# Where the remainder of the token rows is formed, and where the selection of expert slots is built, in a four-layer diffusion trunk step

## What is computed

```python
pg = softmax(xt @ w_rg); p_grp, g_idx = top_k(pg, 1)            # 1 of 4 groups
le = (xt @ w_re) of that group; pe_top, e_idx = top_k(softmax(le), 2)
weight = p_grp * pe_top / sum(pe_top)
hid = silu(xt @ w1[x]) * (xt @ w3[x])
y = sum over experts of (hid * combine) @ w2[x]
```

## Time and profile before

| | |
|---|---|
| median of 3 runs | 1474.15 us (1473.59 to 1474.91) |
| profiled execution | 1473.45 us, of which the span from the first to the last instruction is 1471.7 us |
| TensorE | busy 1370.5 us (93% of the span), mean granted clock 0.981 |
| VectorE, ScalarE, GpSimd | busy 373.4 us (25%), 287.7 us (20%), 61.2 us (4%) |
| transfers | 552.48 MB, 375 GB/s over the span |
| chain that ended last | PE 76%, DMA 18%, DVE 4%, ACT 1%, issue 1% |

### The profile page before, as it was taken

How to read it: one execution, slowest core, us unless ns; L and a number is a source line. 1 busy time by engine, 2 the same in 40 slices (tenths; PEclk the granted TensorE clock), 3 DMA queues, 4 the chain that set the end, 5 groups by cost and what they waited for, 6 DMA issues and landing times.

```text
span 1471.7 us, 17304 instructions
## 1 busy us (share of the span) xinstructions
PE 1370.5 (93%) x7218; PEld 740.3 (50%) x7218; DVE 373.4 (25%) x885; ACT 287.7 (20%) x519; POOL 61.2 (4%) x54
## 2 busy tenths in 40 slices
PE   6999998999989999989999889899999886999986
PEld 3686574444335888754444346544443343444433
DVE  2343514111103322351111121421111134111112
ACT  3211023111102232231111113411110143111102
POOL 1001311000000000020000000200000011000000
PEclk9999999999999999999999999999999997999999
DMA  9945998999999942697999999979999999999994
GB/s 381 419 160 195 404 404 320 384 425 428 428 427 422 421 162 100 277 409 292 428 426 427 428 423 420 421 312 412 426 428 428 425 420 424 428 428 428 425 428 175
DMA packets 54213, 552.48 MB, mean 375 GB/s; under 512 B 5937, under 2 KB 7921, under 8 KB 8817
## 3 DMA queue, kind: packets, MB, share of 16 engines
q1 hardware_dynamic: 52496, 549.29, 89.8%
q10 hardware_dynamic: 1634, 2.02, 0.4%
HBM read 549.19 MB, written 2.10 MB: 375 GB/s over the span
## 4 chain that ended last, share of the span: by engine, by line
PE 76%; DMA 18%; DVE 4%; ACT 1%; issue 1%; POOL 0%; SPq 0%; DVEq 0%; POOLq 0%
PE bank L713 23%; DMA ring<-in_moe_w 16%; PE bank L659 13%; PE bank L737 11%; PE bank L678 4%; PE bank L619 4%; PE bank L696 3%; DMA ring<-in_w_ada 2%; PE bank L492 2%; PE bank L508 2%; PE bank L633 2%; PE bank L833 1%; PE bank L934 1%; PE bank L995 1%; PE bank L569 1%; PE bank L565 1%
## 5 line engine op out<-in xcount | busy, mean ns | idle before, releaser
L713 PE MATMUL bank<-ring,arena 128*64 128x512 f32 x1024 | 230.7, 599 | 31.1 <-DMA ring<-in_moe_w 30.3
L713 PE MATMUL bank<-ring,hT 128*64 128x512 f32 x1024 | 225.3, 594 | 0.0
L737 PE MATMUL bank<-ring,arena 128*64 128x512 f32 x896 | 198.9, 596 | 0.0
L713 PEld LDWEIGHTS bank<-ring,arena 128*64 128x64 f32 x1024 | 73.3, 137 | 180.7 <-issue 150.4
L713 PEld LDWEIGHTS bank<-ring,hT 128*64 128x64 f32 x1024 | 72.1, 137 | 139.3 <-issue 137.3
L1398 DVE TENSOR_TENSOR rows<-rows,bank 128x512 f32<-128x512 f32 x32 | 22.0, 688 | 468.8 <-PE bank L713 468.8
L737 PEld LDWEIGHTS bank<-ring,arena 128*64 128x64 f32 x896 | 61.2, 137 | 117.7 <-issue 112.3
L659 PE MATMUL bank<-hT,ring 128*128 128x256 f32 x512 | 113.4, 384 | 1.7 <-DVE hT L1366 1.7
L659 PEld LDWEIGHTS bank<-hT,ring 128*128 128x128 f32 x512 | 97.8, 192 | 16.0 <-issue 2.7
L1132 ACT ACTIVATE yv_big<-bank,arena 128x512 fp32r<-128x512 f32 x64 | 44.0, 688 | 287.5 <-PE bank L737 287.5
L619 PE MATMUL bank<-ring,condT 128*32 128x512 f32 x768 | 91.8, 606 | 8.2 <-DMA ring<-in_w_ada 6.5
(11 more groups left out here) (213 smaller groups left out, 1273.2 us busy)
## 6 DMA issues: line engine op xcount, KB each, us to landing
ring<-in_moe_w SPq DMA_DIRECT2D x166, 2048.0 KB, 19.2
ring<-in_w_ada SPq DMA_DIRECT2D x96, 1024.0 KB, 21.3
ring<-in_moe_w SPq DMA_DIRECT2D x36, 1024.0 KB, 19.5
arena<-in_moe_w SPq DMA_DIRECT2D x16, 1024.0 KB, 16.8
ring<-in_hy_w_in SPq DMA_DIRECT2D x12, 1024.0 KB, 26.2
ring<-in_hy_w_out SPq DMA_DIRECT2D x4, 1024.0 KB, 12.1
ring<-in_gla_w_v SPq DMA_DIRECT2D x4, 1024.0 KB, 27.8
ring<-in_gla_w_g SPq DMA_DIRECT2D x4, 1024.0 KB, 26.5
```

Source lines behind the costliest of these rows:

```text
L713: last = mm(bank[4 + kind][SLOTS * e:SLOTS * e + SLOTS, :], x[:, k, at:at + SLOTS], w[:, kk, e, :], start=k == 0, stop=k == KD - 1)
L737: last = mm(bank[6 + q // 2][SLOTS * e:SLOTS * e + SLOTS, :], hidT[:, f, SLOTS * e:SLOTS * e + SLOTS], w[:, ff, e, :], start=f == 0, stop= ...
```

## The change

Per layer:

- TensorE writes the transposes as an open accumulation on each bank. After ScalarE has written `htok_big` (one copy of each bank instead of two), TensorE multiplies it by a negated identity `minus` onto the same bank, which leaves bank - big = rest. ScalarE copies the four banks into `htok_rest`. GpSimd's `token_rests` and `htok_raw` are gone. ScalarE builds `minus` once a layer, in `residual`.
- TensorE's four ada pieces are split: two ahead of the rests, one after them, one after the rank matmuls.
- VectorE takes up the ranks directly after `memb` and builds the selection from them; the weights (L1498 to L1507) follow it. The table of slot numbers runs from 1 to 64 instead of 0 to 63, which makes the subtraction of 1 (L1512) superfluous.
- ScalarE's two small exponentials stand behind the first rest copy and behind the last.

```diff
-    base = np.concatenate([np.eye(P), np.tile(np.arange(SLOTS), (P, 1)),
+    base = np.concatenate([np.eye(P), np.tile(np.arange(1, SLOTS + 1), (P, 1)),
...
-        htok_raw = ar(2048, G, D)
+        minus = exact("minus", 5120, P)
... TensorE, moe
-                        last = tr(bank[2 * g + k // 4][:, (k % 4) * P:(k % 4) * P + P], hT[:, k, g], ident)
+                        last = mm(bank[2 * g + k // 4][:, (k % 4) * P:(k % 4) * P + P], hT[:, k, g], ident,
+                                  start=k % 4 == 0, stop=k % 4 == 3, is_transpose=True, skip_group_check=True)
...
-                    ada(beside, 4, 8)
+                    ada(beside, 4, 6)
+                for n in range(4):
+                    pe.wait_ge(s("htok_big"), 4 * i + n + 1)
+                    mm(bank[n][:], minus[:], htok[0][:, n // 2, (n % 2) * 512:(n % 2) * 512 + 512], start=False,
+                       stop=True, skip_group_check=True).then_inc(s("rest_mm"), 1)
+                if beside is not None:
+                    ada(beside, 6, 7)
                 pe.wait_ge(s("members"), i + 1)
...
                 mm(bank[4][:, 32:48], ones16[:], mb[1], start=False, stop=True).then_inc(s("ranks_mm"), 1)
+                if beside is not None:
+                    ada(beside, 7, 8)
                 pe.wait_ge(s("htok_rest"), 4 * (i + 1))
... ScalarE, residual (m == 0)
+                        act.wait_ge(s("base_loaded"), 16)
+                        act_fn(minus[:], ident, ACT.Copy, scale=-1.0)
... ScalarE, moe
-                        for dst in (htok_raw, htok[0]):
-                            last = act_fn(dst[:, g, h * 512:h * 512 + 512], bank[2 * g + h][:], ACT.Copy)
-                        last.then_inc(s("htok_big"), 1)
-
-                    act.wait_ge(s("route_in"), 2 * i + g + 1)
-                    act_fn(*route_exp[g], ACT.Exp).then_inc(s("route_exp"), 1)
+                        act_fn(htok[0][:, g, h * 512:h * 512 + 512], bank[2 * g + h][:], ACT.Copy) \
+                            .then_inc(s("htok_big"), 1)
+                for n in range(4):
+                    act.wait_ge(s("rest_mm"), 4 * i + n + 1)
+                    act_fn(htok[1][:, n // 2, (n % 2) * 512:(n % 2) * 512 + 512], bank[n][:], ACT.Copy) \
+                        .then_inc(s("htok_rest"), 1)
+                    if n == 0:
+                        act.wait_ge(s("route_in"), 2 * i + 1)
+                        act_fn(*route_exp[0], ACT.Exp).then_inc(s("route_exp"), 1)
+                act.wait_ge(s("route_in"), 2 * i + 2)
+                act_fn(*route_exp[1], ACT.Exp).then_inc(s("route_exp"), 1)
... VectorE, moe: these lines move ahead of the weights
+                dve.wait_ge(s("ranks_mm"), i + 1)
+                v.reduce_max(r_mx, bank[4][:, 32:48], AX.X)
+                chain(stt(rank[:], bank[4][:, 0:32].rearrange("p (g e) -> p g e", g=G), 1.0, memb, ALU.add, ALU.mult))
+                build_sel("", 0)
...
-                chain(ts(rank[:], r_rk, -1.0, None, ALU.add))
... GpSimd
-            token_rests(0)
```

More of the change, by code:

```diff
@@ L1507, in moe @@
                          r_wt.unsqueeze(2).broadcast_to([P, G, 4, 4]), ALU.mult))
-                dve.wait_ge(s("ranks_mm"), i + 1)
-                v.reduce_max(r_mx, bank[4][:, 32:48], AX.X)
-                chain(stt(r_rk, bank[4][:, 0:32].rearrange("p (g e) -> p g e", g=G), 1.0, memb, ALU.add, ALU.mult))
-                chain(ts(rank[:], r_rk, -1.0, None, ALU.add))
-                build_sel("", 0)
                 for j in range(3):
@@ L1773, in add_squares @@
                     v.tensor_tensor(hT[:, 0], hT[:, 0], hT[:, k], ALU.add).then_inc(s("squares_added"), 1)
[L1775 to L1781, removed]
             pool.wait_ge(s("skip_loaded"), 16)
@@ L1793, in _ @@
             add_squares(1)
-            token_rests(0)
             add_squares(3)
-            token_rests(1)
             add_squares(5)
-            token_rests(2)
             add_squares(7)
-            token_rests(3)
 def vector_columns(inputs):
```

## The result

The changed kernel takes 1455.1 us (median of 4 runs, 1454.46 to 1455.64) against 1474.53 us for the kernel before beside it: a ratio of 0.9866, with a 95% interval of 0.9852 to 0.9879. The forecast was 1454.8 in a range of 1450 to 1462.5. The profiled execution took 1455.36 us.

What follows compares the result with a forecast made beforehand. The weight stream was taken to set the late pace, with DMA gaps behind routing in layers 0 to 2. Gains of 6.2, 6.4 and 6.7 us, together 19.3, take 1473.45 to 1454.1, plus 0.7: 1454.8 us, range 1450 to 1462.5.

Steps and rivals of the forecast that it cites:

- GpSimd's remainders: VectorE's chain to the membership: four long operations shorten once GpSimd's remainders go, membership 3.49 us earlier.
- The price of 0.17 us for a free operation: VectorE's long operations with two SBUF operands, 0.76 to 1.24 us, priced at 0.17 us without GpSimd's work beside them.
- TensorE's own work: Rest matmuls and ada pieces ahead of the ranks: rests about 0.9 us, third piece ending with the membership, 0.1 us added.
- Selection before weights: VectorE behind the rank matmuls: selection first and no L1512; with the earlier membership, layer 0's gather starts 4.8 us earlier.
- The clock: TensorE's gather: full clock instead of half, 4.0 us long, gaining 1.4, 1.6 and 1.9 us in layers 0 to 2.
- The stream: Weight transfers: gains fit the DMA gaps behind routing in layers 0 to 2; layer 3, without a gap, gains 0.
- The rival that layer 3 pays too: Layer 3's routing gain also reaches the end: 4 layers, about 26 us, 1448 us; chance 0.05.
- The rival that the stream absorbs everything: DMA gaps behind the routing have another cause than the full ring, so no gain: 1474 us; chance 0.03.
- that of another cause of the stall: VectorE's stall isn't GpSimd's; only its order counts, about 3 us in all, 1471 us; chance 0.06.
- that of late rests: Rest matmuls and ScalarE copies on the transposed banks end last, gather 4.7 us late, 1488 us; chance 0.02.
- The sum: Whole kernel: 6.2, 6.4 and 6.7 us in layers 0 to 2, 0 in layer 3, together 19.3 us.

Runs made afterwards that it cites:

- run with reads alone: Changed kernel, with GpSimd again doing four unused 128x512 subtractions beside VectorE's chain in each layer (also called the run with subtractions): 1465.64 us, ratio 0.9945.
- run with memsets: Changed kernel, with GpSimd doing eight 128x512 memsets into an unused tile beside VectorE's chain: 1455.93 us, ratio 0.9873.
- run without tie-breaking: Changed kernel, with each choice of a maximum cut from four VectorE operations to one, so equal scores would choose two: 1455.25 us, ratio 0.9862.
- the rests alone: Changed kernel with the weights ahead of the selection again and slot numbers from 0, the remainders still on TensorE: 1464.85 us, ratio 0.9934.
- the order alone: Kernel before, with only the selection built ahead of the weights from slot numbers 1 to 64; GpSimd still forms the remainders: 1469.77 us, ratio 0.9969.
- the same with two pieces moved: Changed kernel without tie-breaking and with the matmuls of two ada pieces moved, seven between the router's logit matmuls, one behind the transposes: 1455.04 us, ratio 0.9863.
- the run that fills the wait: Kernel before, with TensorE filling its wait for the membership with 15 zero matmuls (30 in layer 3): 1471.71 us, ratio 0.9982.
- the run that delayed it by 3.6 us: Changed kernel with GpSimd's four unused subtractions in layer 3 alone: 1456.6 us, ratio 0.9874.

## Why the prediction was right

**GpSimd's remainders.** Forecast 3.49 us off the membership; measured 9.39 - 5.91 = 3.48 in layer 0, and the same in layers 1 and 2. The price of 0.17 us for a free operation, read from the same line after GpSimd's end, carried it. The run with reads alone brought the stall back without the rest of the old kernel, and the run with memsets did not: together they show the cause.

**TensorE's own work.** This is the term that was too small. I had the ranks start at 6.02; they start at 6.28. The four rests took 1.13 us from 231.49 to the third piece at 232.62, not 0.9. Their spacing was as priced, 0.23 to 0.24 us, but there are 0.33 us behind the first and 0.32 behind the last. The ada pieces around them took a little more, too: the two ahead 1.85 instead of 1.82, the third 1.00 to the ranks instead of 0.91. I wrote that TensorE would be ready just when the membership comes, within 0.1 us. It is 0.37 us late, and the run without tie-breaking shows that it, and not VectorE, sets the time there.

**Selection before weights.** From the start of the ranks to the selection I had 1.32 us, and it is 1.32. Alone, the order brought the gather 1.35 to 1.38 us forward in each of the three layers, against the 1.36 of the forecast, and the median 4.7 us down, 1.6 a layer. One thing I had missed: in its place behind the rest copies, ScalarE's second exponential holds up the weights by 1.0 us, as the run with the rests alone shows. The new order hides it.

**The clock.** Taken as full, and in layers 0 to 2 it was: 4.05 us in the gather, forecast 4.0. From the gather's start to the first expert matmul that is 1.33, 1.51 and 1.84 us less, forecast 1.4, 1.6 and 1.9. In layer 3, where the prediction looked for the same on TensorE, it was not: 0.50 and 5.44 us. It cost nothing there, because nothing in that layer's routing reaches the end. The full clock was also less safe than I had it. In all profiles the clock was full in every gather with 0.2 us of idle time ahead of it. With 1.18 us it fell in most (all four layers of the order alone, layer 3 of the changed kernel) but not in all (layer 3 without tie-breaking, and the same with two pieces moved: 4.05 and 4.06 us), and with 2.3 to 2.5 us it fell in all layers of the rests alone and in two of four in the run that fills the wait. In layers 0 and 2 of the run with subtractions it was at 0.50 though no idle time stood just ahead: it had fallen in the wait for the membership. So the idle time just ahead doesn't decide by itself.

**The stream.** Each layer's gain fitted into the DMA gap behind its routing, and layer 3 gained nothing, to 0.01 us. In all fourteen profiles its experts start between 9.96 and 18.51 us after its first transpose, and from there to the last long piece it is 236.2 to 236.8 us in thirteen of them and 237.3 in one; the earliest and the latest start both have 236.26. The rival that layer 3 pays too fell with that and with the run that delayed it by 3.6 us. The rival that the stream absorbs everything fell with the gaps' going; that of another cause of the stall with the run with reads; that of late rests with the last rest at 6.84, 0.76 us ahead of the selection.

**The sum.** 18.3 us in the three layers against the forecast 19.3: 0.27 us a layer by TensorE's late ranks, 0.07 by the gather. The medians differ by 19.4 us and the profiled executions by 18.1; the start-up was 0.94 us shorter in the profile after, its end 0.9 us longer. So that the forecast is within 0.3 us of the median is in part luck: the sum was 1 us too large, and about 1 us of scatter made up for it.

## What to carry to other kernels

Look at small operations of one line in a timeline: if the same line takes 0.17 us in one place and 1.2 in another, see which engine is busy in between, and whether their ends coincide. Price a gain on the critical engine only after checking the stream's idle gaps behind it: where there is a gap as long as the gain, it goes through, as in layers 0 to 2, and where the stream is closed to the end, as in layer 3 here, it is worth nothing. When a chain gets shorter, add up what the other engine still has to do in the same time, since it is the next bound. And when work is moved into another stage's waits, measure that stage's end as well: here it came 0.6 us later for 0.3 us won behind it.

## What the runs showed that I had not expected

- Eight GpSimd memsets beside the same VectorE operations cost them nothing (0.17 us each), four subtractions cost them 0.77 to 0.99 us each.
- The clock was hard to hold by filling a wait: with the same 15 matmuls and the same 2.5 us of idle time behind them, it stayed at 2.4 GHz in layer 0 and fell to 1.2 GHz in layers 1 and 2. The run with subtractions in four layers spread over 1464 to 1472 us; its two slowest executions have the lowest mean granted clocks (0.984 and 0.986), which fits a clock that falls in more layers of them, but only one has a profile by layer.
- In layer 3 of the changed kernel the gather ran mostly at half clock (5.44 us), and the layer is no longer for it: 236.25 us against 236.26 before.
- Four or seven ada matmuls between the logit matmuls lengthened that stage by the same 0.6 us.
